# Twelve transfers in place of forty-eight for the stacked S5 matrices, and the first two input stacks issued by ScalarE

## The reference

```
bb_re = coef_re[..., None] * b_re - coef_im[..., None] * b_im
bb_im = coef_re[..., None] * b_im + coef_im[..., None] * b_re
bu_re = jnp.einsum('blgc,gpc->blgp', xg, bb_re)
bu_im = jnp.einsum('blgc,gpc->blgp', xg, bb_im)
```

## Time and profile before

| what | us |
|---|---|
| median of 3 runs (lowest, highest) | 1625.79 (1623.38, 1627.77) |
| the profiled execution | 1625.55 |
| its span from first to last instruction | 1624.3 |
| TensorE busy in the span | 1530.6 (94%) |
| VectorE, ScalarE, GpSimd busy | 830.4, 842.1, 284.6 |
| idle time of TensorE ahead of L718, all causes | 48.2 |
| mean granted clock of TensorE | 0.979 |

### The profile page before, as it was taken

One profiled execution on the slowest core, in us unless ns is written; L12 is line 12 of the kernel. 1 busy time (PEld: TensorE's weight loads), 2 busy tenths in 40 slices (PEclk: granted clock), 3 DMA queues, 4 the chain that ended last, 5 costly groups with the idle time before them and its releaser, 6 DMA issues.

```text
span 1624.3 us, 17799 instructions
## 1 busy us (share of the span) xinstructions
PE 1530.6 (94%) x6632; PEld 1196.6 (74%) x6632; DVE 830.4 (51%) x1619; ACT 842.1 (52%) x1074; POOL 284.6 (18%) x316
## 2 busy tenths in 40 slices
PE   6899999999999999999768999888989999999997
PEld 5687788788788888888556676545776888888886
DVE  6778634555587756445233999896345112111011
ACT  5678877844655455454234544762535544444441
POOL 2111111111111111111012213332311111111111
PEclk9999999999999999999879999999999999999999
DMA  8667788799899889998658868535997998888882
GB/s 253 158 152 187 182 192 190 186 314 325 229 247 257 211 212 211 275 250 209 172 140 213 194 178 228 140 109 140 320 302 160 241 234 195 186 189 184 189 184 78
DMA packets 102486, 333.57 MB, mean 205 GB/s; under 512 B 12272, under 2 KB 15344, under 8 KB 102272
## 3 DMA queue, kind: packets, MB, share of 16 engines
q0 software_dynamic: 37856, 137.76, 44.8%
q1 hardware_dynamic: 60720, 187.20, 34.6%
q10 hardware_dynamic: 3824, 7.47, 1.2%
HBM read 179.69 MB, written 18.87 MB: 122 GB/s over the span
## 4 chain that ended last, share of the span: by engine, by line
PE 73%; DVE 12%; ACT 5%; DMA 4%; SPq 2%; issue 2%; POOL 1%; ACTq 0%; DVEq 0%; POOLq 0%
PE ps L718 24%; PE ps L721 23%; PE ps L719 23%; DMA wlo<-raw 2%; SPq L2351 2%; DMA pl_f<-spill 1%; DVE sml L1974 1%; DVE pl_f L1977 1%; DVE pl_f L1923 1%; DVE pl_f L1770 1%; DVE pl_f L1925 1%; ACT whi L1100 1%; ACT wlo L1107 1%; PE ps L995 1%; DVE pl_f L1574 1%
## 5 line engine op out<-in xcount | busy, mean ns | idle before, releaser
L718 PE MATMUL ps<-pl_r,whi 128*128 128x512 f32 x1976 | 791.2, 400 | 48.2 <-ACT pl_r L1134 24.6
L719 PE MATMUL ps<-pl_r,wlo 128*128 128x512 f32 x1976 | 786.0, 398 | 0.0
L721 PE MATMUL ps<-pl_r,whi 128*128 128x512 f32 x1976 | 785.8, 398 | 0.0
L718 PEld LDWEIGHTS ps<-pl_r,whi 128*128 128x128 f32 x1976 | 374.7, 190 | 150.5 <-ACT pl_r L1134 24.5
L721 PEld LDWEIGHTS ps<-pl_r,whi 128*128 128x128 f32 x1976 | 374.1, 189 | 92.4 <-DVE pl_r L1506 1.1
L719 PEld LDWEIGHTS ps<-pl_r,wlo 128*128 128x128 f32 x1976 | 374.6, 190 | 89.2 <-issue 0.5
L2120 POOL DMA_DIRECT2D wlo<-raw x246 | 213.1, 867 | 1142.5 <-ACT wlo L1107 1114.2
L1100 ACT ACTIVATE whi<-raw 128x1024 fp32r<-128x1024 f32 x247 | 260.0, 1053 | 198.1 <-PE ps L721 154.1
L1107 ACT ACTIVATE wlo<-raw 128x1024 fp32r<-128x1024 f32 x246 | 257.0, 1045 | 0.0
L1490 DVE TENSOR_TENSOR pl_r<-pl_f,pl_r 128x512 fp32r<-128x512 f32 x120 | 83.0, 692 | 46.6 <-ACT pl_r L1127 29.6
L2094 DVE TENSOR_TENSOR pl_f<-ps,pl_f 128x512 f32<-128x512 f32 x22 | 15.2, 693 | 177.6 <-PE ps L721 177.6
(11 more groups left out here) (225 smaller groups left out, 1192.5 us busy)
## 6 DMA issues: line engine op xcount, KB each, us to landing
wlo<-raw POOLq DMA_DIRECT2D x246, 512.0 KB, 6.4
raw<-in_w SPq DMA_DIRECT2D x245, 512.0 KB, 5.3
pl_f<-in_mod SPq DMA_DIRECT2D x48, 512.0 KB, 9.8
tab<-pl_f SPq DMA_DIRECT2D x16, 512.0 KB, 6.7
pl_f<-tab POOLq DMA_DIRECT2D x16, 512.0 KB, 6.2
xs<-pl_f SPq DMA_DIRECT2D x16, 256.0 KB, 7.9
pl_f<-xs SPq DMA_DIRECT2D x16, 256.0 KB, 9.4
spill<-pl_f ACTq DMA_DIRECT2D x16, 256.0 KB, 3.8
```

Source lines behind the costliest of these rows:

```text
L718: matmul(out, wh, sr(pair, kk, "hi"), start=start, stop=False)
L719: matmul(out, wl, sr(pair, kk, "hi"), start=False, stop=False)
L721: mm = matmul(out, wh, sr(pair, kk, "lo"), start=False, stop=stop)
```

## The change

The turned matrices in `bt` are ordered otherwise: the row of a partition was (c, j, n), with c real or imaginary, j the quarter and n the state; it becomes (j, c, n). ScalarE and VectorE write `bt` in four pieces of 128 elements 1 KB apart in place of one stretch. A transfer can then carry all four j at once: 12 DMAs of 128 KB in place of 48 of 32 KB, the same 1.5 MB. A source row is one stretch of 4 KB, a destination row four stretches of 1 KB (before: two stretches of 512 B to one of 1 KB). The four semaphores `wst_in0..3` become one. The first two stacks (six DMAs) leave SP and are issued by ScalarE behind its copies of `xs 0..3`: four transfers from `xq 0 hi`, then two from `xq 0 lo`. The places of the tiles stay as they are.

```diff
+    def place_rows(self, part, c):
+
+        return self.sr("bt", part).rearrange("p (j c n) -> p c j n", c=2, j=4)[:, c]
...
-                T.wait_ge(at("wst", j), at("st", s))
-                w = sr("wst", j).rearrange("p (i c n) -> p i c n", i=4, c=2)
-                matmul(b, w[0:96, i, c, :], sr("st", s)[0:96], start=True, stop=True).then_inc(
+                T.wait_ge(at("wst"), at("st", s))
+                matmul(b, k.wst[0:96, j, i, c, :], sr("st", s)[0:96], start=True, stop=True).then_inc(
...
-                act(sr("bt", "hi")[:, S * c:S * c + S], ps("s5_turn", c), ACT.Copy).then_inc(
-                    *done.tick(("bt_hi", c)))
+                act(k.place_rows("hi", c), ps("s5_turn", c).rearrange("p (j n) -> p j n", j=4),
+                    ACT.Copy).then_inc(*done.tick(("bt_hi", c)))
...
+    for part, rows in (("hi", (0, 2)), ("lo", (1,))):
+        A.wait_ge(at("xq", 0, part))
+        for s in (0, 1):
+            if part == "hi":
+                A.wait_ge(*freed("st", s))
+            for h in rows:
+                A.eng.dma_start(sr("st", s)[32 * h:32 * h + 32].bitcast(F32),
+                                sr("xq", 0, part)[32 * s:32 * s + 32].bitcast(F32)).then_inc(
+                    *k.st_in[s].tick(("st", s) if h == 1 else None))
...
-                tt(sr("bt", "lo")[:, half], ps("s5_turn", c), sr("bt", "hi")[:, half].bitcast(F32),
-                   ALU.subtract).then_inc(*done.tick(("bt_lo", c), ("s5_turn", c)))
+                tt(k.place_rows("lo", c), ps("s5_turn", c).rearrange("p (j n) -> p j n", j=4),
+                   k.place_rows("hi", c).bitcast(F32), ALU.subtract).then_inc(
+                   *done.tick(("bt_lo", c), ("s5_turn", c)))
...
-    for j in range(4):
-        for i in range(4):
-            for h, part in enumerate(("hi", "hi", "lo")):
-                dma(sr("wst", j)[32 * h:32 * h + 32, 256 * i:256 * i + 256].rearrange(
-                    "p (c n) -> p c n", c=2).bitcast(F32),
-                    sr("bt", part)[32 * i:32 * i + 32].rearrange(
-                        "p (c j n) -> p c j n", c=2, j=4)[:, :, j, :].bitcast(F32)).then_inc(
-                    *k.wst_in[j].tick(("wst", j) if i == 3 and h == 2 else None))
-        k.wst_in[j].release(("bt", "hi"), ("bt", "lo"))
+    for i in range(4):
+        for h, part in enumerate(("hi", "hi", "lo")):
+            dma(k.wst[32 * h:32 * h + 32, :, i].rearrange("p j c n -> p j (c n)").bitcast(F32),
+                sr("bt", part)[32 * i:32 * i + 32].rearrange("p (j m) -> p j m", j=4).bitcast(
+                    F32)).then_inc(
+                *k.wst_in.tick(("wst",) if i == 3 and h == 2 else None))
+    k.wst_in.release(("bt", "hi"), ("bt", "lo"))
     weights(32)
...
     def s5():
-        stacks(0)
         for s in range(16):
```

More of the change, by code:

```diff
@@ L245, in __init__ @@
         self.ssm_in, self.uk_in, self.ki_in = (sig(n, 16) for n in ("ssm_in", "uk_in", "ki_in"))
-        self.wst_in = [sig(f"wst_in{j}", 16) for j in range(4)]
+        self.wst_in = sig("wst_in", 16)
         self.st_in = [sig(f"st_in{i}", 16) for i in range(8)]
@@ L1287, in scalar_engine @@
             rounded("xq", 0, sb("xs", 0), ("xs", 0))
+    for part, rows in (("hi", (0, 2)), ("lo", (1,))):
[7 more added lines that the diff above has]
+                    *k.st_in[s].tick(("st", s) if h == 1 else None))
+    for s in (0, 1):
+        k.st_in[s].release(("xq", 0, "hi"), ("xq", 0, "lo"))
     def s5():
@@ L1871, in vector_engine @@
             for c in range(2):
-                half = slice(S * c, S * c + S)
                 V.wait_ge(at("bt_hi", c), *freed("bt", "lo"))
-                tt(sr("bt", "lo")[:, half], ps("s5_turn", c), sr("bt", "hi")[:, half].bitcast(F32),
-                   ALU.subtract).then_inc(*done.tick(("bt_lo", c), ("s5_turn", c)))
+                tt(k.place_rows("lo", c), ps("s5_turn", c).rearrange("p (j n) -> p j n", j=4),
+                   k.place_rows("hi", c).bitcast(F32), ALU.subtract).then_inc(
+                   *done.tick(("bt_lo", c), ("s5_turn", c)))
     r2, b = k.factor(3, 0, 4), ps("sums", 3)
@@ L2474, in build @@
                             for n, c in (("ssm_b", 2), ("ssm_c", 3)))
+        k.wst = k.place(k.book.home["wst", 0][0], 8)[1].rearrange(
+            "p (j i c n) -> p j i c n", j=4, i=4, c=2)
         k.uk = k.sb("uk").rearrange("p (c n) -> p c n", c=2)
```

## The result

| | us |
|---|---|
| before, median of 4 runs (lowest, highest) | 1624.59 (1623.14, 1627.77) |
| after, median of 4 runs (lowest, highest) | 1601.63 (1598.97, 1604.05) |
| ratio, 95% interval | 0.9856 (0.9831 to 0.9880) |
| profiled execution of after, its span | 1603.27, 1602.0 |
| predicted | 1596.0, range 1590.5 to 1607.0 |

The profiled executions differ by 22.3 us, against a forecast sum of 29.8. A later set of runs, where before took 1628.24 us, gave 1600.67 us for after, 27.6 us less. Lines have moved: L2351 is now L2365, the six issues on ScalarE are L1298, L1134 is L1137, L718 is L722, L902 is L905, L925 is L928 and L2120 is L2135.

What follows compares the result with a forecast made beforehand. TensorE was taken to bound the kernel, with only its stands and half-clock stretches to win. Copies 21.7, clock 0 and stacks 8.1 us made 29.8 us off 1625.55, plus 0.24 for the median: 1596.0 us, range 1590.5 to 1607.

Steps and rivals of the forecast that it cites:

- What bounds the kernel: TensorE stands 24.0 us at L718 for SP's 48 issues, and 5.9 us at L902 for stacks queued behind raw loads.
- Writing `bt` in pieces: ScalarE and VectorE writing `bt`: at most +1.2 and +1.4 us, covered by TensorE's `w_down`, so no cost.
- Twelve for 48: Copies ahead of L1134 and L718: fewer issues, landing at 802.9, TensorE restarting at 803.8; 21.7 us saved, 17.0 to 23.2.
- The start: First of the twelve copies on SP: stays at 791.62, hanging on `wst`'s old users.
- The issues: Twelve copies on SP: 0.64 us each whatever their bytes or pieces, the twelfth starting at 799.60.
- The landing behind the last issue: Last 128 KB copy into SBUF: 3.3 us, with bounds of 1.8 and 8.0 us.
- Rival A: SP's twelve issues: 1.28 us each, reaching beyond 806, only 14.9 us saved there; 1602.8 us in all, chance 0.10.
- The clock: TensorE's restart after a 2.5 us gap: clock stays up, +1.3 us, or half clock follows, -0.3 to -2.0; taken as 0.
- Stacks on ScalarE: First stacks at L902: 5.9 us of wait and 2.2 us of half clock go, 8.1 us saved; lower bound nothing.
- rival B: Stacks at L902 bring nothing, the wait and half clock stay: 21.7 us saved in all, 1604.1 us, chance 0.10.
- Rivals C and D: C: weights run dry behind restart, 1632 us, chance 0.02; D: another event holds ScalarE, 1620 to 1626 us, chance 0.03.
- The sum: Whole kernel: 21.7 + 0 + 8.1 = 29.8 us saved, with work behind 880 us moving as a whole.

Runs made afterwards that it cites:

- The parts alone: Two kernels: the twelve copies with the first stacks left on SyncE, 1606.47 us; 48 copies with the first two stacks issued by ScalarE, 1618.32 us.
- own places: The changed kernel with the places of `bt` given back only behind the norm, so no tile of `u` lies on them: 1591.69 us, ratio 0.9785.
- after again: The changed kernel run and profiled once more, nothing altered, also called the second profile: 1600.67 us, ratio 0.9833.
- the add moved: The changed kernel with the rounding and 512 KB `wlo` add of unit 136 moved behind ScalarE's second tile of `u`: 1597.57 us, ratio 0.9832.
- the two queues: The changed kernel with six of the twelve copies issued by SyncE and six by ScalarE: 1602.36 us, ratio 0.9841.
- filled gap: The changed kernel with about 7 us of unused matmuls put into TensorE's gap ahead of the second tile of `u`: 1600.93 us, ratio 0.9835.

## Why the prediction came out as it did

**What bounds the kernel.** Right: both places, their causes and the order behind them. The parts alone and the own places show it: the wait is for places, the stacks wait for a raw load.

**Writing `bt` in pieces.** Right: no wait came of it.

**Twelve for 48.** The path was right, the size wrong: 21.7 us forecast, 18.05 measured in after and 19.0 in after again. The landing came at 806.63 and not at 802.9, a difference of 3.7 us with three terms.

The start, +1.5 us: it was put at 791.62 since it "hangs on `wst`'s old users"; it also hangs on the raw load ahead of it in the same queue, which held it 1.9 us behind the sums in after. In the second profile the load cost nothing, and the start is 0.5 us later only because the sums are.

The issues, +2.8 us, the term that failed most: "Nothing grows with bytes or pieces, so I keep 0.64 a piece". For an issue by itself that is right, 0.60 us at 128 KB with the add moved. What it left out is what else moves at that time. The twelve copies bring 107 to 117 us of engine time, 6.7 to 7.3 us on all 16, into the 8.6 us in which they were to be issued, the add brings 3 us more and the raw loads 2.7 to 3.4. With the add moved it is 7.6 us from first to last issue, where 8.0 were forecast and 10.8 measured in after, so moving it took away all of this term. I had the busy share in front of me (a quarter beside the 48 copies) and didn't scale it to copies issued four times as densely.

The landing behind the last issue, -0.6 us: 2.68 against 3.3.

**Rival A** (an issue costs by what it carries) gave 1602.8 us, nearer to the 1601.6 measured than the forecast's 1596.0, but by the wrong cause: with the add moved an issue of 128 KB takes 0.60 us, and with 24 copies of 64 KB it takes 0.6 us whatever its pieces. Of the signs named for it neither came: the issues ended at 804.55, past the 801 of the forecast and short of the 806 of the rival. So that the measured time lies within the forecast's own range of 1590.8 to 1602.7 us, at its slow end, is owed to the wide bound on the landing (8.0 us) and not to a term for the other transfers, which the forecast didn't have.

**The clock.** Taken as 0 between -2.0 and +1.3. In after twelve matmuls of the restart fell into half clock in place of six or seven: about -1.0 us. The gap that stayed was 7.3 us and not 2.5, so this follows from the start and the issues. With the add moved a gap of 1.35 us stayed, and the clock was full behind it: the upper one of the two cases.

**Stacks on ScalarE.** Right, 8.1 us forecast: 5.90 us of wait and 2.26 us of clock measured, 8.16. The issues cost 622 ns in the middle case (590 forecast) and landed in 5.5 us (3.3), against a cover that held. GpSimd's `wlo` add of unit 140 went out 29.0 us behind the restart (27.7 forecast) and nobody waited for it. The Trainium skill, page "DMA: Bandwidth & Descriptors", section "Issuing engines are not separate DMA queues", was the sentence beside rival B. It speaks of the time to initiate alone; for the stacks the 7.0 us measured alone were SyncE's wait ahead of the issue and the clock behind the gap, of which it says nothing. No run here tests it for the twelve copies, since the two queues issued them one after the other.

**Rivals C and D** didn't come: no wait for `wlo` in the stage, and ScalarE started 0.08 us behind the last landing.

**The sum.** 21.7 + 0 + 8.1 = 29.8 forecast; 18.05 - 1.0 + 5.9 + 2.3 = 25.2 in the stage. Behind it 2.9 us net were lost again in the first profile and none in the second, where the stage's 26.5 us ended as 27.5. "Work behind 880 us is taken to move as a whole" holds to about 3 us, by where the half-clock stretches fall.

## What to carry to other kernels

When a wait is for a transfer, ask first whether it is for its data or for the places it reads: here 7 to 9 us were left for nothing but the order in which places were handed out. When small transfers are merged, sum their time on the DMA engines over the shorter time in which they will now be issued, together with whatever else runs there; if it fills that time, the gain ends there. Here moving the 512 KB add brought 3 us of landing; whether a second issuing engine would bring any is not shown. A transfer in a strictly ordered queue is as late as the wait of its predecessor, and moving it to a queue whose predecessors are done gave the whole wait here, 5.9 us, and the 2.3 us of clock lost behind it.

## What the runs showed of the hardware

An issue of a copy inside SBUF took 0.60 us in the middle case on SyncE, whether it carried 32 KB, 64 KB or, with the add moved, 128 KB, in 64 or 128 pieces. Beside the packets of a 512 KB accumulating transfer issued by GpSimd, two or three of the issues of 128 KB took 1.5 to 2.1 us, on SyncE and on ScalarE; with the engines 0.96 busy but without that transfer none did. A piece of 1 KB inside SBUF occupied a DMA engine for 65 to 73 ns, one of 512 B for 27 to 34 ns in the middle case, so bytes and not pieces set this time at these two sizes. A 4 KB packet of the accumulating transfer took 327 to 345 ns, one of a raw load 159 ns. A gap of 7.3 us on TensorE was followed by 5.5 us of work at half clock, one of 1.35 us by none, and full clock through a filled gap was seen once.
